# The first pair's tokens by a product on chip in place of a gather, a shorter choice chain, and one weight buffer loaded in another order

## The reference, cut to what matters

```python
def hier_moe(h, rg_w, rg_b, re_w, re_b, w_gate, w_up, w_down):
    lg = tf @ rg_w + rg_b
    pg = jax.nn.softmax(lg, axis=-1)
    grp = jnp.argmax(lg, axis=-1)
    g1 = jnp.take_along_axis(pg, grp[:, None], axis=-1)
    le_all = jnp.einsum('td,gde->tge', tf, re_w) + re_b
    le = jnp.take_along_axis(le_all, grp[:, None, None], axis=1)[:, 0]
    top_v, top_i = lax.top_k(le, TOP_K_INNER)
    g2 = jax.nn.softmax(top_v, axis=-1)
    eid = grp[:, None] * EXPERTS_PER_GROUP + top_i
    combine = jnp.sum(jax.nn.one_hot(eid, N_EXPERTS) * (g1 * g2)[..., None], axis=1)
    for e in range(N_EXPERTS):
        hid = jax.nn.silu(t @ w_gate[e]) * (t @ w_up[e])
        acc = acc + combine[:, e:e + 1] * (hid @ w_down[e])
```

## Time and profile before

| | |
|---|---|
| median of 3 runs | 792.37 us (791.98 to 793.82) |
| span of the profiled execution | 789.4 us |
| its own time | not listed; the three runs lie 2.6 to 4.5 us above its span |
| mean granted TensorE clock | 0.987 |
| PE busy | 757.8 us (96%) |
| DMA moved | 249.58 MB, mean 316 GB/s |
| logits done to first gate product | 316.5 to 332.95 us |
| experts | 332.95 to 778 us |

### The profile page before, as it was taken

One profiled execution on the slowest core, in us unless ns is written; L12 is line 12 of the kernel. 1 busy time (PEld: TensorE's weight loads), 2 busy tenths in 40 slices (PEclk: granted clock), 3 DMA queues, 4 the chain that ended last, 5 costly groups with the idle time before them and its releaser, 6 DMA issues.

```text
span 789.4 us, 8694 instructions
## 1 busy us (share of the span) xinstructions
PE 757.8 (96%) x3470; PEld 360.5 (46%) x3470; DVE 270.5 (34%) x629; ACT 154.4 (20%) x308; POOL 140.3 (18%) x168
## 2 busy tenths in 40 slices
PE   6999999999999999799999999999999999989896
PEld 4667677767843335434333333333333333333332
DVE  2399499985656423511101101110110011011003
ACT  3211121245712003202011112101111110110122
POOL 2279998612002000100000000000000000000000
PEclk9999999999999999799999999999999999999998
DMA  9990610042659786999999999999999999999982
GB/s 312 304 364 10 230 40 1 9 107 108 188 213 275 252 306 237 368 374 414 429 426 427 425 429 425 425 430 426 427 427 426 425 426 427 427 429 425 429 356 69
DMA packets 51400, 249.58 MB, mean 316 GB/s; under 512 B 6982, under 2 KB 24422, under 8 KB 38671
## 3 DMA queue, kind: packets, MB, share of 16 engines
q1 hardware_dynamic: 45460, 243.40, 77.2%
q10 hardware_dynamic: 3371, 2.81, 1.2%
q0 software_dynamic: 2528, 2.79, 1.1%
HBM read 246.87 MB, written 8.61 MB: 324 GB/s over the span
## 4 chain that ended last, share of the span: by engine, by line
PE 91%; DMA 3%; DVE 2%; SPq 2%; issue 2%; ACT 1%; POOLq 0%; DVEq 0%
PE bank L1213 28%; PE bank L810 18%; PE bank L1236 14%; PE bank L1076 9%; PE bank L1261 9%; DMA xcx<-in_state_conf_conv 2%; PE bank L1196 2%; SPq L491 1%; PE bank L1225 1%; PE bank L1065 1%; PE bank L1034 1%; PE bank L905 1%; PE bank L1214 1%; PE bank L1122 1%; PE bank L1047 0%
## 5 line engine op out<-in xcount | busy, mean ns | idle before, releaser
L810 PE MATMUL bank<-region_a,ring 128*128 128x320 f32 x576 | 157.2, 433 | 1.0 <-DMA ring<-in_w_in 1.0
L1654 DVE TENSOR_TENSOR region_a<-region_a,bank 64x512 f32<-64x512 f32 (+1 forms) x33 | 22.5, 680 | 377.6 <-ACT region_a L1581 377.6
L1214 PE MATMUL bank<-ring,zz 128*64 128x512 f32 x320 | 145.4, 610 | 0.0
L1213 PE MATMUL bank<-ring,zz 128*64 128x512 f32 x288 | 127.3, 595 | 2.7 <-issue 2.7
L810 PEld LDWEIGHTS bank<-region_a,ring 128*128 128x128 f32 x576 | 108.7, 190 | 46.3 <-DVE region_a L1654 1.1
L1655 DVE SCALAR_TENSOR_TENSOR bank<-region_a,par,bank 128x256 f32<-128x256 f32 x232 | 91.2, 479 | 0.0
L763 POOL DMA_INDIRECT region_a<-hn_scratch,region_a x16 | 15.9, 996 | 369.6 <-PE bank L1196 355.8
L1261 PE MATMUL bank<-zz,masks 128*128 128x512 f32 (+1 forms) x192 | 77.2, 603 | 0.7 <-ACT zz L1587 0.7
L1213 PEld LDWEIGHTS bank<-ring,zz 128*64 128x64 f32 x288 | 38.1, 137 | 82.5 <-issue 81.7
L1076 PE MATMUL bank<-ring,x_v_y 128*128 128x512 f32 (+1 forms) x192 | 74.0, 605 | 0.0
L1581 ACT ACTIVATE region_a<-bank 64x512 f32<-64x512 f32 x32 | 18.9, 590 | 271.5 <-PE bank L1214 271.5
(11 more groups left out here) (313 smaller groups left out, 770.1 us busy)
## 6 DMA issues: line engine op xcount, KB each, us to landing
ring<-in_expert_w_up SPq DMA_DIRECT2D x20, 2048.0 KB, 24.4
ring<-in_expert_w_gate SPq DMA_DIRECT2D x17, 2048.0 KB, 30.3
ring<-in_expert_w_down SPq DMA_DIRECT2D x16, 2048.0 KB, 34.8
ring<-in_w_in SPq DMA_DIRECT2D x9, 2048.0 KB, 15.7
x_v_y<-in_expert_w_down SPq DMA_DIRECT2D x6, 2048.0 KB, 33.5
x_v_y<-in_expert_w_gate SPq DMA_DIRECT2D x5, 2048.0 KB, 34.6
ring<-in_w_out SPq DMA_DIRECT2D x4, 2048.0 KB, 10.0
xcx<-in_expert_w_gate SPq DMA_DIRECT2D x4, 2048.0 KB, 31.8
```

The costliest lines, as they stand in the source:

```text
L810: ins = pe.matmul(pt[0:m, 0:T], w[:, k, :], ht[:, k, :], start=k == 0, stop=k == KD - 1)
L1213: pe.matmul(to[0:CAP, :], x[:, k, :], wg[:, FE * k:FE * k + FE], **st)
L1214: ins = pe.matmul(to[CAP:P, :], x[:, k, :], wu[:, FE * k:FE * k + FE], **st)
L1654: tt_ = lambda out, a, b, op: dve.tensor_tensor(out, a, b, op)
```

## The change

- The job "first", its index and the first gather are gone, and so is `gath_begun`. PE makes the first pair's tokens itself, already transposed, as the product of the normed rows `hn` (stationary, 128 columns of a stride of 8) with `first` (128 columns moving): 2 halves x 4 blocks x 3 tiles of tokens. POOL begins with the second pair's gather.
- The last residual product stands ahead of this product in PE's order, and `slot_values` behind it. The banks of these jobs are turned by one.
- In `first_max` three fused operations, one for each tile, become two plain ones over all tiles. Two subtractions that only feed the softmax (`g_in`, `e_in`) move behind `chosen`.
- On DVE the place of each token and `osel` are made ahead of the combine weights, and the two `tokens(0, h)` stand ahead of the reading of the slots.
- SP loads the tenth unit's second half straight behind the eighth unit, and its first half once `xg_T` is 2, that is when PE has read `hn` for the last time. The eleventh unit stands behind it.

```diff
@@ -327,7 +327,7 @@
         r3 = lambda t: t.rearrange("p (r n) -> p r n", r=3)
         lg = r3(moe(3 * 36))
         ee = moe(2 * 3 * NE).rearrange("p (o u e) -> p o u e", o=2, u=3)
-        tee = moe(2 * 3 * NE).rearrange("p (o u e) -> p o u e", o=2, u=3)
+        tee = zf[:, D:D + 2 * 3 * NE].rearrange("p (o u e) -> p o u e", o=2, u=3)
         aa = r3(moe(3 * NE))
         og, sg4, t4 = (r3(moe(3 * NG)) for _ in range(3))
         le, o1, o2, s8, t8 = (r3(moe(3 * EG)) for _ in range(5))
...
@@ -335,7 +335,8 @@
         at[0] = UNIT + 1024
         cols = moe(3 * 16).rearrange("p (n r) -> p n r", r=3)
         val = moe(2 * 3 * 2 * NE).rearrange("p (o u c e) -> p o u c e", o=2, u=3, c=2)
-        osel = zf[:, 0:2 * 3 * CAP].rearrange("p (o u s) -> p o u s", o=2, u=3)
+        osel, osel_more = (zf[:, c0:c0 + 2 * 3 * CAP].rearrange("p (o u s) -> p o u s", o=2, u=3)
+                           for c0 in (D + 2 * 3 * NE, 0))
         first = zf[:, 2048:2048 + 3 * P].rearrange("p (u s) -> p u s", u=3)
         first_off, first_at = (zf[:, 2048 + 3 * P + 6 * b:2048 + 3 * P + 6 * b + 6].rearrange("p (u j) -> p u j", u=3)
                                for b in range(2))
...
@@ -356,7 +357,7 @@
         b_gu, b_t, b_dn = bank[0], bank[1], bank[2]
 
         def job_bank(kind, at):
-            return bank[M[kind, at] % 3]
+            return bank[(M[kind, at] + 2) % 3]
 
         def job_free(pe, kind, at):
...
@@ -364,7 +365,7 @@
             n = M[kind, at]
             if n >= 3:
                 pe.wait_ge(S(MOE_JOBS[n - 3][2]), MOE_JOBS[n - 3][3])
-            return bank[n % 3]
+            return bank[(n + 2) % 3]
 
         acc = bank[3:8]
         M_SSUM, M_G1, M_M1, M_M2, M_E, M_R, M_W1, M_W2, M_S1, M_S2, M_T, M_D = range(12)
...
@@ -553,17 +554,17 @@
             for m in range(4, R):
                 slot_free(N_MIX + m)
                 load_expert(m + 2)
-            sp_.wait_ge(filled, J[("lg2",)] + 1)
-            load_expert(n_slot - 3)
 
             def load_half(j, h, sem):
                 part = slice(UNIT // 2 * h, UNIT // 2 * h + UNIT // 2)
                 sp_.dma_start(e_slot[j % n_slot][:, part], expert_src(*EXPERT[j])[:, part]).then_inc(sem, 16)
 
+            load_half(n_slot - 2, 1, S("tenth_half"))
+            sp_.wait_ge(filled, J[("lg2",)] + 1)
+            load_expert(n_slot - 3)
             sp_.wait_ge(S("hn_out"), 48)
-            load_half(n_slot - 2, 0, S("tenth_half"))
-            sp_.wait_ge(S("gath_begun"), 1)
-            load_half(n_slot - 2, 1, expert_in[n_slot - 2])
+            sp_.wait_ge(S("xg_T"), 2)
+            load_half(n_slot - 2, 0, expert_in[n_slot - 2])
             sp_.wait_ge(S("kept"), 1)
             load_expert(n_slot - 1)
...
@@ -758,15 +759,13 @@
 
                 pool.tensor_tensor(wait_word[:, w:w + 1], halfrow, halfrow, ALU.add)
 
-            for i in range(NE // 2):
-                wait(pool, S("xg_T"), 2 * i)
+            for i in range(1, NE // 2):
+                if i > 1:
+                    pool.wait_ge(S("xg_T"), 2 * i)
                 pool.indirect_dma_start(gat, None, hn_dram[:, :],
                                         bass.IndirectOffsetOnAxis(ap=gpair[:, i:i + 1], axis=0),
                                         bounds_check=T - 1, oob_is_err=False).then_inc(S("gath"), 16)
-                if i == 0:
-                    pool.memset(wait_word[:, 0:1], 0.0).then_inc(S("gath_begun"), 1)
-                    pool.wait_ge(S("idx"), 2)
-            pool.wait_ge(S("gath"), 16 * (NE // 2))
+            pool.wait_ge(S("gath"), 16 * (NE // 2 - 1))
 
             over = pool.value_load(mcount[0:1, 0:1], min_val=0, max_val=T)
             with pool.If(over > CAP):
...
@@ -1165,15 +1164,23 @@
             counts(ones, 2, 3, start=False, stop=True).then_inc(filled, 1)
             residual(2)
 
+            residual(1, [1]).then_inc(S("kept"), 1)
+
+
+            pe.wait_ge(S("hn"), 3)
             pe.wait_ge(S("first"), 1)
-            pt = take(pe, "first")
-            for r in range(3):
-                n = TILES[r][1]
-                ins = pe.matmul(pt[:, 0:1], first[0:n, r, :], tokid[0:n, r:r + 1], start=r == 0, stop=r == 2)
-            ins.then_inc(filled, 1)
-            residual(1, [1]).then_inc(S("kept"), 1)
-
-            def slot_values(pt):
+            after_read(pe, "h2", 2, 1)
+            after_read(pe, "lg2")
+            for h in range(2):
+                to = job_bank("tokens", (0, h))
+                for k in range(4):
+                    for r in range(3):
+                        n = TILES[r][1]
+                        ins = pe.matmul(to[:, P * k:P * k + P], hn[0:n, r, 4 * h + k:D:KD], first[0:n, r, :],
+                                        start=r == 0, stop=r == 2)
+                ins.then_inc(S("xg_T"), 1)
+
+            def slot_values(pt, osel):
                 for n_, (r, w) in enumerate([(r, w) for r in range(3) for w in range(2)]):
                     n = TILES[r][1]
                     for h in range(2):
...
@@ -1183,8 +1190,7 @@
                 return ins
 
             pe.wait_ge(S("osel"), 1)
-            slot_values(take(pe, "slots")).then_inc(filled, 1)
-            after_read(pe, "first")
+            slot_values(take(pe, "slots"), osel).then_inc(filled, 1)
             pe.wait_ge(free["act"], len([1 for _, who in JOBS if who == "act"]))
...
@@ -1279,9 +1285,6 @@
             def combine_rest(i):
                 to_tokens(back[i % 2], yo_of, PARTS[-1:]).then_inc(S("added"), 1)
 
-            pe.wait_ge(S("gath"), 16)
-            for h in range(2):
-                tokens_T(0, h)
             after_read(pe, "slots")
 
             for i in range(NE // 2):
...
@@ -1294,7 +1297,7 @@
                     gate_up(to, xgt[:, :, own_half[e % 2]], gate, up, first=e == 0).then_inc(S("gu_done"), 1)
                 more = i + 1 < NE // 2
                 if more:
-                    pe.wait_ge(S("gath"), 16 * (i + 2))
+                    pe.wait_ge(S("gath"), 16 * (i + 1))
                     for h in range(2):
                         tokens_T(i + 1, h)
                 if i >= 2:
...
@@ -1921,15 +1924,13 @@
             def first_max(vals, w, mx, out, desc, tmp_):
 
                 link(dve.tensor_reduce(col(mx), vals, AX.X, ALU.max))
-                for r in range(3):
-                    ins = stt(tmp_[:, r, :], vals[:, r, :], col(mx)[:, r:r + 1], desc, ALU.is_equal, ALU.mult)
-                link(ins)
+                link(tt_(tmp_, vals, wide(mx, w), ALU.is_equal))
+                link(tt_(tmp_, tmp_, bc(desc.unsqueeze(1), [P, 3, w]), ALU.mult))
                 link(dve.tensor_reduce(col(M_T), tmp_, AX.X, ALU.max))
                 link(tt_(out, tmp_, wide(M_T, w), ALU.is_equal))
 
             groups = lg[:, :, 0:NG]
             first_max(groups, NG, M_SSUM, og, desc4, t4)
-            tt_(sg4, groups, wide(M_SSUM, NG), ALU.subtract).then_inc(S("g_in"), 1)
             by_group = lambda t: t.rearrange("p r (g e) -> p r g e", g=NG)
             of_group = bc(og.unsqueeze(3), [P, 3, NG, EG])
             link(tt_(by_group(t32), by_group(lg[:, :, NG:]), of_group, ALU.mult))
...
@@ -1937,16 +1938,17 @@
             first_max(le, EG, M_M1, o1, desc8, s8)
             link(stt(le, o1, -3.0e38, le, ALU.mult, ALU.add))
             first_max(le, EG, M_M2, o2, desc8, s8)
-            tt_(col(M_D), col(M_M2), col(M_M1), ALU.subtract).then_inc(S("e_in"), 1)
             in_group = lambda t: bc(t.unsqueeze(2), [P, 3, NG, EG])
             link(tt_(s8, o1, o2, ALU.add))
             tt_(by_group(aa), in_group(s8), of_group, ALU.mult).then_inc(S("chosen"), 1)
-
+            tt_(sg4, groups, wide(M_SSUM, NG), ALU.subtract).then_inc(S("g_in"), 1)
+            tt_(col(M_D), col(M_M2), col(M_M1), ALU.subtract).then_inc(S("e_in"), 1)
             for w, oo in enumerate((o1, o2)):
                 ins = tt_(by_group(ee[:, w]), in_group(oo), of_group, ALU.mult)
             link(ins)
+            dve.wait_ge(S("chosen"), 1)
+            dve.tensor_scalar(first_off, aa[:, :, 0:2], -BIG, BIG, ALU.mult, ALU.add).then_inc(S("first_off"), 1)
             places_of = cols[:, M_S1:M_S2 + 1, :]
-            dve.tensor_scalar(first_off, aa[:, :, 0:2], -BIG, BIG, ALU.mult, ALU.add).then_inc(S("first_off"), 1)
             pt = got(dve, "rank")
             dve.wait_ge(S("first_off"), 1)
             link(tt_(first_at, r3(pt[:, 0:3 * NE])[:, :, 0:2], first_off, ALU.add))
...
@@ -1955,28 +1957,33 @@
             dve.tensor_copy(cnt, pt[:, 3 * NE:4 * NE])
             tt_(tee, ee, bc(r3(pt[:, 0:3 * NE]).unsqueeze(1), [P, 2, 3, NE]), ALU.mult).then_inc(free["dve"], 1)
             tt_(val[:, :, :, 0, :], ee, bc(tokid.unsqueeze(1).unsqueeze(3), [P, 2, 3, NE]), ALU.mult)
+            after_read(dve, "rank")
+            link(dve.tensor_reduce(places_of, tee, AX.X, ALU.add))
+
+            def slot_select(osel):
+                return tt_(osel.rearrange("p o u s -> p (o u) s"), bc(slotno.unsqueeze(1), [P, 6, CAP]),
```

(32 more changed lines are left out.)

13 lines of the change are left out of this document (4 added, 9 removed).

## The result

The changed kernel takes 802.89 us, median of 4 runs (802.39 to 805.76), where the kernel before takes 793.1 in the same comparison. The ratio is 1.0124, with a 95% interval from 1.0097 to 1.0151. It is slower by some 10 us; forecast was no change, with 796.0 as the upper end. The profiled execution took 802.86 us, and its span is 801.1.

What follows compares the result with a forecast made beforehand. The weight stream was taken to bound the experts' end. Stream -0.1 us, not cut by PE's 0.6 lead, plus 0.2 for the upper start gave +0.1 on the median 792.37: 792.5, own range 791.0 to 793.9, with rivals 790.4 to 796.0.

Steps and rivals of the forecast that it cites:

- the price of the new product: First pair's tokens on PE: 24 products, 48 instructions at 0.115 us, 5.5 us, ending at 330.4.
- 10.8 us: Upper bound for the new token product on PE, at the lower clock with about 0.225 us per instruction.
- The choice: DVE's choice ahead of the ranks: plain operations and moved subtractions save 0.6 us together, bounds 0.3 and 0.8.
- The ranks: After DVE's choice: start at 321.2 in place of 321.82, keep their 1.66 us and end at 322.9.
- The residual products: On PE ahead of the new product: tile 2's takes 1.00 us, the last, moved here, about 0.87, until 324.7.
- The slots: `slot_values` on PE right behind the new product: 1.6 us, lower bound 0.9, ending at 331.9.
- The wait: PE waits for DVE to read the slots, formerly hidden by the gather: 1.3 us, then gates at 333.2.
- The stream: Weight transfers before 360: stand still until `xg_T` plus a start, restart at 331.9, reach the same bytes at 349.1, -0.1 us.
- PE's lead of up to 7 us in the middle: In the middle of the experts, PE can be up to 7 us ahead or behind the weight stream at no price.
- The clock stays low in part of the product: Rival in the new token product: half of it at low clock costs 2.7 us, giving 795.2; chance 0.22.
- The whole product takes 11 us: Rival in the new token product: +5.3 us, 797.7; chance 0.06 by the clock, 0.02 by the page's f32 price.
- The clock falls elsewhere later: Rival at the last pairs: the half-clock stretch behind the last wait is spared, 1.7 us faster, 790.8; chance 0.20.

Runs made afterwards that it cites:

- the probe of the strides: Changed kernel with the first pair's token product replaced by f32 products reading at strides 1, 2, 4 and 8, results not the reference's; 796.31 us.
- the contiguous versions: Changed kernel with ScalarE writing the normed rows in blocks, so products read at stride 1: 795.24 us; with the product's tile and block loops exchanged too: 792.28 us.
- the grouped one: Changed kernel, operand still at stride 8, with the product's tile and block loops exchanged for fewer row-count changes; 802.0 us, ratio 1.0101.
- the probe of the row counts: Changed kernel with the first pair's token product replaced by groups of 128 rows, 64 rows or both in turn, results not the reference's; 805.54 us.

## Why the prediction was wrong

**The step that failed** is the price of the new product, "48 instructions x 0.115 = 5.5 us", and with it the bound, "10.8 us", that was to hold if the clock stayed low. It measured 15.27 us. The price was read from a product that shared type, columns and instruction count with the new one, but had both operands contiguous and one row count. The bound was wrong in the same way: it varied the clock, the one thing for which the trace had two rows, and not the access. What the runs showed in its place is 11.5 us for 48 instructions at stride 8, 2.9 for 15 changes of the row count, and 0.9 for the half clock. By the probe, a strided operand takes 0.24 at full clock already, so a full clock could never have brought 5.5.

**The choice** saved 0.48 us (from the last logit work at 317.06 to the ranks at 321.91, 4.85; before 5.33), forecast 0.6. All of this execution's chain up to there was 0.57 later than in the one before. **The ranks** kept their 1.66. **The residual products** took 2.06, forecast 1.87 (four times 0.23 would have been 0.92 for the second, not 0.87).

**The slots** took 1.67, forecast 1.6. That is luck: they ran at half clock, as in the kernel before, while the forecast was at the full clock, where they take 0.99 in the contiguous versions. **The wait** for DVE behind them was 1.36, forecast 1.3, and was right.

**The stream** was right as a rule and applied to a wrong time. By the forecast's own arithmetic, each us by which `xg_T` comes later moves the end by one. It came at 340.9 in place of 330.4, 10.5 us; 792.5 + 10.5 = 803.0, and 802.89 was measured. That this meets to 0.1 is luck, since the spans of the two traces are 11.7 apart and the clock moved both ends. With contiguous rows `xg_T` came at 336.7, 6.3 late, and the last wait ended 5.9 later than in the kernel before; with grouped tiles too it came at 331.8, 1.4 late, the last wait ended 0.8 later, and the time was 792.28, the forecast. The cover that the prediction named, PE's lead of up to 7 us in the middle, did not help, since the stream itself lost the time.

**The rivals.** "The clock stays low in part of the product" has the right sign and the wrong size and place. The clock was full when the product began and fell at 330.68, in the middle of it, while PE ran without a gap; that cost some 0.9 us in the product. Then the slots and the first gates ran at half clock until 347.7, which delayed the buffers they free and left the hole of 350 to 352, another 0.9 us; in the versions with contiguous rows, at the full clock, there is none. The reason given against this rival, that PE has much more to do there, did not hold. "The whole product takes 11 us" was nearer, but neither of its two reasons holds. The estimate from the page (the Trainium skill, TensorE: Matmul & The Clock Gate, Terms), 11.0 us, comes near the 11.5 of 48 strided instructions by coincidence: a contiguous f32 product took 2 x 0.11 to 0.12 us in the probes, and a transpose 1.02 / 8 = 0.13, so the factor is under two and not four. "The clock falls elsewhere later" is a real mechanism and happened: in the changed kernel the clock fell at 719.9, ahead of the last pair and not behind it, and from that pair's start to the end are 49.9 us, where the kernel before has 51.7. It was hidden under the larger loss.

**What it was said to be wrong by** was right: "if the product takes over 7 us". The waits of the last four pairs did not stay within 1 us either: 1.57, 2.69, 3.20 and none, against 1.90, 0.47, 2.69 and 1.99.

## What to carry to other kernels

A price read from a row holds for the row's access too: before a product is costed by another, compare the strides of both operands and the row counts of its neighbours, not only type, shape and clock. A one-hot product in place of a gather is no loss here only when its operand lies contiguous and tiles of one height are worked together; it then costs 5.9 us, and gave no gain until the slots and a load were moved too. A queue's hole may be what a small transfer lives on, so look at who runs behind it before it is filled. And a low clock costs where nothing else is waited for: ahead of a wait it was hidden, behind the last one it cost its whole 1.7 us.

## What the runs showed of the hardware

- f32 products with an operand at a stride of 4 or 8 elements take 0.23 to 0.24 us per instruction of 128 columns, against 0.11 to 0.12 at a stride of 1 or 2; stationary or moving makes no difference. With 256 columns the strided stationary took 0.257. Transposes hardly feel it: eight took 1.08 us with the stationary operand at stride 8, and 1.02 contiguous.
- A change between 128 and 64 rows from one product to the next costs 0.19 us at the full clock and 0.25 to 0.29 at half; 64 rows alone cost what 128 do.
- The granted clock fell from 1.00 to 0.50 at 330.68 in the changed kernel, at 333.3 in the grouped one and at 336.4 in the probe of the row counts, each time in products that followed each other without a gap and read at stride 8. In the probe of the strides, with 30 such instructions, and inside the products from contiguous rows it did not fall. What exactly makes it fall is open.
- ScalarE's copy of 1024 columns took 2.25 us with its input read at a stride of 8, against 1.15 contiguous.
- A gather of 128 rows took 3.83 and 3.21 us right behind a pause of the stream, 8.73 and 9.98 without the pause, and 10.7 in the median later on.
